# Indexer queries projected with one matmul per product over the 392 token columns that are used

## What is computed

```python
IN_WIDTHS = (ATTN_WIDTH, ATTN_WIDTH, ATTN_WIDTH, IDX_HEADS * IDX_DIM, IDX_DIM, IDX_HEADS, POOL_WIDTH, D_MODEL, D_MODEL)
p = jnp.einsum('btd,dn->btn', z, w_in)          # z: (b, t, 2048)
q, k, v, qi, ki, wi, u, ga, gb = jnp.split(p, bounds, axis=-1)
...
def indexer_scores(qi, wi, ki):
    s = jnp.einsum('bthi,bsi->bths', qi, ki) * (IDX_DIM ** -0.5)
    return jnp.einsum('bths,bth->bts', jax.nn.relu(s), wi)
...
topk = min(TOPK_MAX, t // 4)                     # 128 for the prompt
sc = jnp.where(causal, indexer_scores(qi_blk, wi_blk, ki), -jnp.inf)
_, idx = lax.top_k(sc, topk)
```

## Time and profile before

| | us |
|---|---|
| Median of 3 runs | 2986.35 |
| Lowest and highest | 2985.96, 2988.5 |
| Profiled execution | 2986.26 |
| Its span | 2984.5 |
| TensorE busy in it | 2889.8 |
| VectorE busy in it | 1417.5 |
| Mean granted TensorE clock | 0.991 |

### The profile page before, as it was taken

The page is one execution under the profiler, slowest core; times in us unless marked ns, Lnnn a source line. Parts: engine busy times, 40 slices in busy tenths (PEclk is TensorE's granted clock), DMA queues, the critical chain, the costliest instruction groups (busy, mean ns, idle before and its releaser), DMA issues.

```text
span 2984.5 us, 54377 instructions
## 1 busy us (share of the span) xinstructions
PE 2889.8 (97%) x23119; PEld 2811.7 (94%) x23119; DVE 1417.5 (47%) x2186; ACT 863.9 (29%) x1055; POOL 858.7 (29%) x280
## 2 busy tenths in 40 slices
PE   6999999999999999999989999999999999999997
PEld 6988999989899988999989999999989999999997
DVE  4544765536364603331147777777762322222312
ACT  4123222122222213323333444444332222222212
POOL 3332332323234642433310000000024444444441
PEclk9999999999999999999999999999999999999999
DMA  5321332222234743334324434433453233323321
GB/s 184 107 72 58 126 96 75 86 65 85 68 99 156 253 160 127 127 124 131 127 78 142 135 117 138 134 125 129 141 213 129 99 115 114 114 100 111 130 100 58
DMA packets 268699, 354.18 MB, mean 119 GB/s; under 512 B 9706, under 2 KB 199346, under 8 KB 267225
## 3 DMA queue, kind: packets, MB, share of 16 engines
q1 hardware_dynamic: 232067, 296.01, 30.2%
q10 hardware_dynamic: 29262, 30.28, 3.1%
q0 software_dynamic: 7200, 25.30, 2.5%
HBM read 310.55 MB, written 41.19 MB: 118 GB/s over the span
## 4 chain that ended last, share of the span: by engine, by line
PE 85%; issue 6%; DVE 4%; POOL 2%; ACT 1%; DMA 1%; DVEq 1%; ACTq 0%; POOLq 0%; SPq 0%
PE PP L1801 57%; PE PP L2153 17%; PE AB L2153 3%; PE AB L1811 3%; POOL lo L1090 2%; PE AB L1986 1%; PE AB L2044 1%; DMA qb<-q_scratch 1%; PE AB L1979 1%; DVE prod L1513 1%; PE AB L1871 0%; DVE craw L1720 0%; ACT AB L743 0%; DVE scS L1448 0%; DVE lo L1612 0%
## 5 line engine op out<-in xcount | busy, mean ns | idle before, releaser
L1090 POOL TENSOR_TENSOR lo<-raw,hi 128x2048 fp32r<-128x2048 f32 x168 | 798.0, 4750 | 1991.6 <-ACT hi L722 1310.8
L1801 PE MATMUL PP<-zh,hi 128*128 128x260 f32 x2336 | 501.9, 296 | 13.7 <-issue 11.7
L722 ACT ACTIVATE hi<-raw 128x2048 fp32r<-128x2048 f32 x168 | 321.2, 1912 | 636.5 <-PE PP L1801 618.1
L1801 PE MATMUL PP<-zh,lo 128*128 128x260 f32 x2336 | 473.2, 284 | 0.0
L1801 PE MATMUL PP<-zl,hi 128*128 128x260 f32 x2336 | 473.1, 284 | 0.0
L1801 PE MATMUL PP<-fh,hi 128*128 128x260 f32 x2048 | 415.0, 284 | 10.5 <-POOL lo L1090 5.0
L1801 PE MATMUL PP<-fh,lo 128*128 128x260 f32 x2048 | 414.5, 284 | 2.3 <-issue 2.3
L1801 PE MATMUL PP<-fl,hi 128*128 128x260 f32 x2048 | 413.9, 284 | 0.0
L1801 PEld LDWEIGHTS PP<-zh,hi 128*128 128x128 f32 x2336 | 362.8, 191 | 42.4 <-issue 35.7
L1801 PEld LDWEIGHTS PP<-zh,lo 128*128 128x128 f32 x2336 | 363.6, 190 | 0.0
L1801 PEld LDWEIGHTS PP<-zl,hi 128*128 128x128 f32 x2336 | 363.3, 190 | 0.0
(11 more groups left out here) (381 smaller groups left out, 5190.2 us busy)
## 6 DMA issues: line engine op xcount, KB each, us to landing
raw<-in_w_in_dram SPq DMA_DIRECT2D x36, 2048.0 KB, 8.3
raw<-in_w_up_dram SPq DMA_DIRECT2D x32, 2048.0 KB, 9.3
raw<-in_w_down_dram SPq DMA_DIRECT2D x32, 2048.0 KB, 8.0
ffn_scratch<-stg SPq DMA_DIRECT2D x32, 520.0 KB, 2.8
craw<-ffn_scratch SPq DMA_DIRECT2D x16, 1040.0 KB, 6.4
raw<-in_w_out_dram SPq DMA_DIRECT2D x8, 2048.0 KB, 10.0
gates_scratch<-gst ACTq DMA_DIRECT2D x32, 260.0 KB, 3.6
raw<-in_w_attn_out_dram SPq DMA_DIRECT2D x8, 1024.0 KB, 5.8
```

Source lines behind the costliest of these rows:

```text
L722: act.activation(part(hi, kind, u), raw_unit(kind, u), ACT.Copy).then_inc(hi_done, 1)
L1090: pool.tensor_tensor(part(lo, kind, u), raw_unit(kind, u), part(hi, kind, u).bitcast(F32), ALU.subtract)\
L1801: mm = pe.matmul(PP[:, slot, f, 0:HC], w[:, k, P * e:P * e + P], a[:, f, :], start=(k == 0 and n == 0), stop=(k == nk - 1 and n == 2))
```

## The change

The eight units of the indexer queries no longer go through `unit` but through a new function `index_unit`. It reads columns 128 to 519 of the 520 (`QI_COLS`, 392 columns) in one matmul, across the border of the two halves, in place of 260 and 260. A product is one matmul in place of two, a unit 48 in place of 96. The first 128 prompt tokens get no indexer queries. The result lies in the first bank of the slot of `PP` alone: 128 prompt columns, 4 sample columns, 256 prompt columns, 4 sample columns. ScalarE's copy and VectorE's subtraction are each split in two (128 and 256 columns), and VectorE's copies of the sample columns take them from their new places. Waits, hooks and their places, weight loads and splits stay.

```diff
+    QI_COLS = slice(P, 2 * HC)
+    QI_N = 2 * HC - P
+    QI_PROMPT = ((slice(P, HP), slice(0, HP - P)), (slice(HP, SEQ), slice(HC - P, HC - P + HP)))
+
+    def qi_sample(rows, slot):
+
+        few = HC - HP
+        return PP[rows, slot, 0, HP - P:QI_N].rearrange("p (a b) -> p a b", b=few)[:, 0:HC // few + 1:HC // few, :]
+
...
         def queries_high(j):
             act.wait_ge(pe_halves, 2 * (2 * N_QI + j + 1))
-            act.activation(qih[:, j, :].rearrange("p (f c) -> p f c", f=2), PP[:, j % 2, :, 0:HP], ACT.Copy)\
-                .then_inc(s_qih, 1)
+            for to, cols in QI_PROMPT:
+                ins = act.activation(qih[:, j, to], PP[:, j % 2, 0, cols], ACT.Copy)
+            ins.then_inc(s_qih, 1)
...
             dve.wait_ge(s_qih, j + 1)
-            dve.tensor_tensor(halves(qil[:, j, :]), PP[:, u % 2, :, 0:HP], halves(qih[:, j, :]).bitcast(F32),
-                              ALU.subtract)
-            dve.tensor_copy(qiB[0:HD, 0, 0, j, :].rearrange("p (f c) -> p f c", f=2), PP[0:HD, u % 2, :, HP:HC])
-            dve.tensor_copy(qiB[HD:P, 1, 1, j, :].rearrange("p (f c) -> p f c", f=2), PP[HD:P, u % 2, :, HP:HC])\
+            for to, cols in QI_PROMPT:
+                dve.tensor_tensor(qil[:, j, to], PP[:, u % 2, 0, cols], qih[:, j, to].bitcast(F32), ALU.subtract)
+            dve.tensor_copy(qiB[0:HD, 0, 0, j, :].rearrange("p (f c) -> p f c", f=2), qi_sample(slice(0, HD), u % 2))
+            dve.tensor_copy(qiB[HD:P, 1, 1, j, :].rearrange("p (f c) -> p f c", f=2), qi_sample(slice(HD, P), u % 2))\
                 .then_inc(drained[u % 2], 1)
...
+        def index_unit(u, hooks):
+
+            pe.wait_ge(lo_done, u + 1)
+            h_w, l_w = part(hi, "wide", u), part(lo, "wide", u)
+            pe.wait_ge(drained[u % 2], before(u)[u % 2])
+            for k in range(KD):
+                mh, ml = (t.rearrange("p f c -> p (f c)")[:, QI_COLS] for t in z(k))
+                for n, (w, a) in enumerate(((h_w, mh), (h_w, ml), (l_w, mh))):
+                    mm = pe.matmul(PP[:, u % 2, 0, 0:QI_N], w[:, k, :], a, start=(k == 0 and n == 0),
+                                   stop=(k == KD - 1 and n == 2))
+                if k == KD - 1:
+                    mm.then_inc(pe_halves, 2)
+                if k in hooks:
+                    hooks[k]()
+
...
-            unit(2 * N_QI + j, "wide", z, before(2 * N_QI + j), hooks=hooks)
+            index_unit(2 * N_QI + j, hooks)
```

## The result

| | before | after |
|---|---|---|
| Median, in the comparison of the two | 2987.43 us (4 runs) | 2965.39 us (4 runs) |
| Lowest and highest | 2985.96, 2988.63 | 2960.95, 2970.93 |
| Ratio, with its 95% interval | | 0.9927 [0.9908, 0.9946] |
| Profiled execution, its span | 2986.26, 2984.5 us | 2960.95, 2959.2 us |

The change makes the kernel faster by 22.0 us. The forecast was 2963.6 us, 22.7 less than before.

What follows compares the result with a forecast made beforehand. TensorE alone was taken to set the pace, busy 97% of the span. Saving 23.0 us on products plus 0.1 on the first unit, less 0.4 for one wait, gave 2986.3 - 22.7 = 2963.6 us, range 2958.5 to 2970.

Steps and rivals of the forecast that it cites:

- The price before and after: TensorE, indexer query units: a product falls from 0.237 us (two 260-column matmuls) to 0.177 (one of 392; 0.1735 to 0.1835).
- The sum: Whole kernel: 384 cheaper products save 23.0 us, first unit adds 0.1, one wait costs 0.4; 22.7 us saved.
- Drain: ScalarE copies and VectorE subtractions after a unit: at most 0.1 us more each, covered before the next index step; cost 0.
- splits: Splitting the next unit's weights on GpSimd and ScalarE: still done in time for the shorter units; cost 0.
- the later stages: Selection, gates units and attention loop: start 23 us sooner and keep their length and slack.
- The new wait: Second unit, first index step: TensorE waits for VectorE's two `poolT` operations, 0.4 us, once.
- the rival that the load holds 260 columns: TensorE: the weight load, not columns, sets 0.1187 us a matmul; 24.6 us less 0.3 saved, 2962.0 us; chance 3%.
- The clock: TensorE's granted clock falls only after a stop; one fall more or less is possible, plus or minus 3.4 us.
- The dear matmul: TensorE: wide matmuls with 128 weight rows cost more than index steps' with 64; 2984 us, halfway 2974; chance 5%.
- the caught drain: VectorE's `qil` gets held behind GpSimd's split, index steps wait 5.5 us a unit, 38 us: 3002 us; chance 4%.
- the gain given back later: At the hand-over to the attention loop the saving is lost to work fixed in time: 2986 us; chance 3%.
- The cheaper change into a step: TensorE: changing into and out of index steps gets cheaper too, another 4.2 us saved: 2959 us; chance 4%.

Runs made afterwards that it cites:

- the two comparisons: The change against the kernel before: first 2965.39 us against 2987.43, then unedited again 2965.05 us against 2987.97, ratio 0.9928.
- the pairs: Against the changed kernel, the six index steps of a unit put in three hooks of two: 2949.90 us, ratio to before 0.9878.

## Why the prediction was right

- **The price before and after.** Forecast 0.177 us for 392 columns, measured 0.1775, well inside the bounds of 0.1735 and 0.1835.
- **The sum.** Forecast 22.7 us, measured 22.8 in the stretch and 22.0 and 22.9 in the two comparisons. The units came out at 8.53, 18.12 and 14.06 us for the forecast 8.5, 18.1 and 14.0.
- **The base was low.** The kernel before took 2987.4 us in the comparison and not 2986.3. That is 1.1 of the 1.8 us by which 2965.4 lies above 2963.6; the other 0.7 are the gain of 22.0 in place of 22.7, less than the spread of the runs.
- **What was costed at nothing.** Drain, splits and the later stages cost nothing, as said. The extra instructions of the drain cost less than the 0.1 us a unit put down for them: two `qih` copies take 0.55 us (one took 0.60), two `qil` 0.62 (0.69).
- **The new wait.** Forecast 0.4 us. The step starts 0.83 us after the last product (173.43 us), where 0.27 is usual, so 0.56 us, once.
- **One reason was incomplete.** The prediction said that the columns set the pace "and not the load". For 260 columns that is so only just: they cost 0.1187 us, and the floor lies at 0.112. So the rival that the load holds 260 columns was nearer than its 3% said. It didn't matter to the sum, because the change takes away a load together with the columns. It would have mattered to an edit that leaves out the columns alone: by the slope of 0.441 ns it would gain 21 us, and it gained nothing (0.9998). The rows of 256 columns and more on which the argument stood can't show a floor that lies just below 256. The trace of the kernel before had a hint: eight matmuls with 32 moving columns in plain float32 (line 1929, from 330.55 us) stand 0.10 us apart, (0.98 - 0.28) / 7.
- **The clock.** "It falls only after a stop of TensorE" was wrong as a rule. In the kernel with 128-column matmuls it fell while TensorE was busy all the time: TensorE had no stop from 182 us on, the clock was 1.00 until 188, and then (us, PE busy, clock):

```profile
191.00:211.00 20.00, 20.00 (x69) 0.50 0.34 106
```

- **The rivals.** The dear matmul, the caught drain and the gain given back later didn't come. The cheaper change into a step didn't come by itself: behind a step two products take 185.35 - 184.90 = 0.45 us against 0.355 usually, 0.1 us as before. Fewer changes can be had, by pairing the steps.

## What to carry to other kernels

A matmul in a row of matmuls with weights of their own costs the larger of two things here: its moving columns (0.45 ns each, 0.230 us for 512) and a floor that goes with its weight columns (0.112 us for 128). They meet at about 0.112 / 0.00045 = 250 columns, an estimate. Near that point neither fewer columns nor fewer matmuls gains anything alone; only both together did. So price an edit by both terms, and look for rows below the crossing before saying which one holds. And where small matmuls use half of the weight rows, let those of the two halves take turns: here it took 1.3 us off each unit beyond the pairs.

## What the runs showed of the hardware that was not expected

- Matmuls in rows 0 to 63 and 64 to 127 of the array, writing different banks, run beside each other when they are issued in turns: two of 512 columns in 0.24 us, where one alone takes 0.23.
- The granted clock fell to half (0.50 from 191 to 211 us) under 128-column matmuls with full weight loads and no idle time, so that this kernel, with a third of the columns in most of its products, took 2986 us in all. A 128-column matmul then costs (194.28 - 192.15) / 10 = 0.213 us: the floor doubles when the clock halves. With half of the weight columns, and each step 0.059 us, the clock stayed at 1.00 between 200 and 270 us. What decides it stays open; each is one run.
- A hook of 64-row matmuls costs TensorE 0.4 us beside its own matmuls and the usual distance to the next product. In the changed kernel the products around a hook start at 188.02 and 188.83 us: 0.81 us, less 0.35 for three matmuls of 256 columns and 0.18 for a product, makes 0.28. The product behind the hook is 0.29 us ahead of the next in place of 0.18, another 0.11.
